# Gathering the tokens of a mixture-of-experts group in two halves of four experts, the second half behind gate and up of the first expert

## The reference

```python
def hierarchical_moe(x, w_group, b_group, w_router, b_router, w_gate, w_up, w_down):
    ...                                        # one group of 4, two experts of its 8, their weights
    combine = (group_onehot[:, :, None] * exp_w[:, None, :]).astype(x.dtype)
    y = jnp.zeros_like(xt)
    for g in range(N_GROUPS):
        h = jax.nn.silu(jnp.einsum('td,edf->tef', xt, w_gate[g])) * jnp.einsum('td,edf->tef', xt, w_up[g])
        y = y + jnp.einsum('tef,efd->td', h * combine[:, g, :, None], w_down[g])
    return y.reshape(B, S, D)
```

## Time and profile before

| | us |
|---|---|
| median of 3 runs | 1186.68 (1186.46 to 1187.39) |
| the profiled execution, its own time | 1187.27 |
| its span, first to last instruction | 1185.4 |
| PE busy | 877.0 (74%) |
| ACT busy | 239.7 (20%) |
| DVE busy | 208.7 (18%) |
| POOL busy | 18.9 (2%) |

### The profile page before, as it was taken

One profiled execution on the slowest core, in us unless ns is written; L12 is line 12 of the kernel. 1 busy time (PEld: TensorE's weight loads), 2 busy tenths in 40 slices (PEclk: granted clock), 3 DMA queues, 4 the chain that ended last, 5 costly groups with the idle time before them and its releaser, 6 DMA issues.

```text
span 1185.4 us, 18548 instructions
## 1 busy us (share of the span) xinstructions
PE 877.0 (74%) x7870; PEld 498.0 (42%) x7870; DVE 208.7 (18%) x516; ACT 239.7 (20%) x555; POOL 18.9 (2%) x38
## 2 busy tenths in 40 slices
PE   8999998668566856685677999866765676567655
PEld 4788564235223522352235556423422342234222
DVE  1022231120012001200112432212010201020112
ACT  2165432112001200120011324101200120012001
POOL 0000000000000000000001100000000000000000
PEclk9999999888889888988888999988988998899789
DMA  9922169999999999999999405999999999999994
GB/s 390 419 107 80 63 235 409 427 428 425 427 427 426 427 426 428 427 426 427 428 425 412 171 20 216 417 425 428 426 428 426 428 425 429 426 427 425 428 426 177
DMA packets 31054, 433.80 MB, mean 366 GB/s; under 512 B 3440, under 2 KB 3568, under 8 KB 4592
## 3 DMA queue, kind: packets, MB, share of 16 engines
q1 hardware_dynamic: 30816, 431.85, 86.8%
q10 hardware_dynamic: 144, 0.52, 0.1%
HBM read 431.31 MB, written 1.05 MB: 365 GB/s over the span
## 4 chain that ended last, share of the span: by engine, by line
DMA 46%; PE 44%; issue 4%; ACT 3%; DVE 2%; DVEq 0%; ACTq 0%; SPq 0%; POOLq 0%; POOL 0%
DMA ring<-in_w_moe 45%; PE ps L1278 9%; PE ps L1266 7%; PE ps L1149 5%; PE ps L1134 4%; PE ps L1322 4%; PE ps L1254 3%; PE ps L1109 2%; PE ps L1346 2%; PE ps L1078 2%; PE ps L1409 1%; ACT xT L645 1%; PE ps L1312 1%; PE ps L1227 1%; PE ps L1372 1%
## 5 line engine op out<-in xcount | busy, mean ns | idle before, releaser
L1278 PE MATMUL ps<-ring,xT 128*32 128x256 f32 x4096 | 283.9, 428 | 156.1 <-DMA ring<-in_w_moe 149.6
L1278 PEld LDWEIGHTS ps<-ring,xT 128*32 128x32 f32 x4096 | 135.8, 120 | 292.7 <-DMA ring<-in_w_moe 190.5
L1322 PE MATMUL ps<-ring,scr 128*32 128x256 f32 x2048 | 137.7, 414 | 39.0 <-DMA ring<-in_w_moe 26.7
L938 DVE TENSOR_TENSOR scr<-scr,ps 128x128 f32<-128x128 f32 x64 | 18.4, 288 | 536.6 <-ACT scr L653 536.6
L1322 PEld LDWEIGHTS ps<-ring,scr 128*32 128x32 f32 x2048 | 69.0, 118 | 92.2 <-ACT scr L655 32.9
L1266 PE MATMUL ps<-scr,xn 128*128 128x256 f32 x256 | 77.7, 468 | 38.7 <-issue 38.1
L653 ACT ACTIVATE scr<-ps 128x128 f32<-128x128 f32 x64 | 17.8, 278 | 382.2 <-PE ps L1278 382.2
L945 DVE COPY scr<-ps 32x256 f32<-32x256 f32 x128 | 53.3, 416 | 215.6 <-PE ps L1322 214.7
L659 ACT ACTIVATE scr<-ps 32x256 f32<-32x256 f32 x128 | 48.2, 377 | 178.0 <-PE ps L1322 177.3
L1266 PEld LDWEIGHTS ps<-scr,xn 128*128 128x128 f32 x256 | 58.6, 239 | 60.2 <-issue 47.4
L1254 PE MATMUL ps<-scr 128*128 128x512 f32 x128 | 62.0, 616 | 8.2 <-ACT scr L659 8.2
(11 more groups left out here) (142 smaller groups left out, 535.2 us busy)
## 6 DMA issues: line engine op xcount, KB each, us to landing
ring<-in_w_moe SPq DMA_DIRECT2D x192, 2048.0 KB, 32.8
ring<-in_w_a SPq DMA_DIRECT2D x7, 2048.0 KB, 28.0
ring<-in_w_b SPq DMA_DIRECT2D x4, 2048.0 KB, 40.0
ring<-in_w_a SPq DMA_DIRECT2D x2, 1024.0 KB, 9.0
h<-in_x SPq DMA_DIRECT2D x2, 512.0 KB, 4.7
ring<-in_w_b SPq DMA_DIRECT2D x1, 1024.0 KB, 41.1
out<-xn SPq DMA_DIRECT2D x4, 256.0 KB, 2.8
par<-in_small SPq DMA_DIRECT2D x1, 768.0 KB, 15.7
```

The lines of the kernel that those rows point to most:

```text
L1278: last = MM(ps[CAP * j:CAP * (j + 1), e % 2, 0:2 * P].rearrange("p (u f) -> p u f", u=2), xg[:, kk, CAP * e:CAP * (e + 1)], w[:, :, k, P * ...
L1322: last = MM(ps[CAP * c:CAP * (c + 1), 2 + b, 0:256], hT[:, b, CAP * j:CAP * (j + 1)], w[:, j, 256 * c:256 * (c + 1)], start=j == 0, stop=j ...
```

## The change

PE gathers four experts at a time: a block of the gather is now 128 columns wide, and there are 2 x 8 blocks in a group. The order on PE becomes: blocks 0 to 3 of experts 0 to 3, `gate_up(0, 0)`, blocks 4 to 7 of experts 0 to 3, `gate_up(0, 1)`, all eight blocks of experts 4 to 7, the transposes of `selw`, then expert 0's transpose and down and the other experts as before. ACT makes 16 copies of 128 columns in place of 8 of 256, still ahead of the copy to `selT` and of the first Silu. DVE builds `selg` in four instructions of 128 x 128 in place of two of 128 x 256, and signals after each pair.

```diff
@@ ACT, group
-                    for k in range(KD):
-                        act.wait_ge(xg_psum, it * KD + (k + 1))
-                        nc.scalar.activation(xg[:, k, :], ps[:, 6 + k % 2, 0:NE * CAP], ACT.Copy,
+                    for i in range(2 * KD):
+                        q, k = i // KD, i % KD
+                        act.wait_ge(xg_psum, it * (2 * KD) + (i + 1))
+                        nc.scalar.activation(xg[:, k, P * q:P * (q + 1)], ps[:, 6 + i % 2, 0:P], ACT.Copy,
                                              scale=gain[:, gi, k:k + 1]).then_inc(xg_done, 1)
                     act.wait_ge(selt_psum, it + 1)
@@ DVE, group
-                    slots = bc(iota.unsqueeze(1), 1, NE)
-                    for t in range(T):
-
-                        last = V.tensor_tensor(selg[:, t, :].rearrange("p (e s) -> p e s", e=NE),
-                                               slots, bc(rank[:, t, cols].unsqueeze(2), 2, CAP),
-                                               ALU.is_equal)
-                    last.then_inc(selg_done, 1)
-                    dve.wait_ge(selg_done, it + 1)
+                    slots = bc(iota.unsqueeze(1), 1, QUAD)
+                    for q in range(2):
+                        quad = bass.ds(g * NE + QUAD * q, QUAD)
+                        for t in range(T):
+                            last = V.tensor_tensor(
+                                selg[:, t, P * q:P * (q + 1)].rearrange("p (e s) -> p e s", e=QUAD),
+                                slots, bc(rank[:, t, quad].unsqueeze(2), 2, CAP), ALU.is_equal)
+                        last.then_inc(selg_done, 1)
+                    dve.wait_ge(selg_done, it * 2 + 2)
@@ PE, group
-                    pe.wait_ge(selg_done, it + 1)
                     pe.wait_ge(xn_done, T * (layer + 2))
-                    def gather(ks):
+                    def gather(q, ks):
+                        pe.wait_ge(selg_done, it * 2 + (q + 1))
                         for k in ks:
-                            if k >= 2:
-                                pe.wait_ge(xg_done, it * KD + (k - 1))
+                            i = KD * q + k
+                            if i >= 2:
+                                pe.wait_ge(xg_done, it * (2 * KD) + (i - 1))
                             for t in range(T):
-                                last = MM(ps[:, 6 + k % 2, 0:NE * CAP], xn[:, t, P * k:P * (k + 1)],
-                                          selg[:, t, :], start=t == 0, stop=t == T - 1)
+                                last = MM(ps[:, 6 + i % 2, 0:P], xn[:, t, P * k:P * (k + 1)],
+                                          selg[:, t, P * q:P * (q + 1)], start=t == 0, stop=t == T - 1)
                             last.then_inc(xg_psum, 1)
@@ PE, group, the order
-                    gather(range(KD // 2))
-                    pe.wait_ge(xg_done, it * KD + KD // 2)
+                    gather(0, range(KD // 2))
+                    pe.wait_ge(xg_done, it * (2 * KD) + KD // 2)
                     gate_up(0, 0)
-                    gather(range(KD // 2, KD))
+                    gather(0, range(KD // 2, KD))
+                    pe.wait_ge(xg_done, it * (2 * KD) + KD)
+                    gate_up(0, 1)
+                    gather(1, range(KD))
                     pe.wait_ge(selw_done, it + 1)
                     ...
-                    pe.wait_ge(xg_done, it * KD + KD)
                     for e in range(NE):
                         b = e % 2
+                        if e == QUAD:
+                            pe.wait_ge(xg_done, it * (2 * KD) + 2 * KD)
                         if e:
                             keep_warm(e, 0)
                             gate_up(e, 0)
                             keep_warm(e, 1)
-                        gate_up(e, 1)
+                            gate_up(e, 1)
```

## The result

| | kernel before | changed kernel |
|---|---|---|
| median | 1183.71 us (14 runs, 1179.51 to 1187.39) | 1189.68 us (14 runs, 1185.18 to 1193.42) |
| profiled execution, its own time | 1187.27 | 1188.93 |
| its span | 1185.4 | 1187.0 |

The ratio is 1.0052, 95% interval 1.0037 to 1.0068: the change costs 6.2 us (4.4 to 8.0). The forecast was 6.4. The two profiled executions differ by only 1.7 us; single executions of one kernel scatter over some 8 us, so the time of one is no measure here. What the profiles are good for is the distances within a stage, which repeat to a tenth of a us.

The account below looks back on a forecast made before the run. The weight stream, by its restart in each layer's first group, was taken to bound the kernel. Later load 3 (2.1) plus clock (1.1) gave 3.2 us a layer, 6.4 for two; on median 1186.7 that is 1193.1, range 1188.0 to 1196.5.

Parts of the forecast that it names:

- What bounds the kernel: MoE layers: weight stream at 427 GB/s bounds; each us on its virtual start is a us on the layer's end.
- The gather's own time and its pace: First group's gather: narrow blocks take 1.19 us a pair (bounds 0.89 and 1.37); PE's own time stays.
- rival (d): Narrow gather on PE: weight loads don't overlap, 0.25 us a record, + 9 us a layer, 1207; chance 0.02.
- What is moved: Expert 0, first group: Silu and table load lose their cover, load 3 issued at 187.8; +2.1 us a layer.
- Rival (c): First group: Silu or table load runs ahead of the last copies; each layer gains 3.0 us, 1180.7; chance 0.06.
- The table's price: ACT before expert 0's Silu: table load takes 1.28 us, the switch at most 0.2 beyond it.
- Rival (e): ACT, first Silu: table switch takes twice 1.28 us, load 3 1.3 later in either layer, 1195.7; chance 0.04.
- The clock: PE's gap before expert 0's down: clock falls, 1.1 us on down in each layer; bounds 0 and 1.4.
- Rival (a): Expert 0's down: the stall without the clock's fall, 2 x 2.1 us, 1190.9; chance 0.26.
- The model of the load: Stream restart: virtual start is the largest, over n, of issue n + 1.8 - 4.91 (n - 1).
- the spare time: Third load, layer 0: could be issued at 185.6 without moving the stream's start; 1.6 us to spare.
- The later groups: Groups after the first: five us later costs nothing, 19 are left; no hole in the stream.

Follow-up runs that it names:

- the kernel with 16 idle matmuls: Kernel before, plus 16 idle matmuls on PE ahead of expert 0's down in every group; ratio 1.0107, 12.7 us longer.
- the kernel with Silu early: Changed kernel with expert 0's Silu and its table load ahead of the second half's copies on ACT; ratio 0.9986 to the kernel before.
- (6): Kernel before, plus 6 idle matmuls on PE ahead of expert 0's down; ratio 0.9991, and 0.9994 when run again.
- the kernel with expert 0 first: Changed kernel with the gather of experts 4 to 7 and its copies moved behind expert 0's down; ratio 0.9961 to the kernel before.
- the split: Moved gather of experts 4 to 7 halved: four blocks behind expert 0's down, four behind expert 1's; ratio 0.9961 to the kernel before.

## Why the prediction was right, point by point

**What bounds the kernel.** Right in the main. The restart of the stream moved, and the sum of lags gives the time within the interval in nearly every kernel run. It also holds that a us of lag is a us on the layer's end: in layer 1, from the gather's start to the last down, the changed kernel takes 444.8 us where the kernel before takes 442.5, and its lag is 2.5 longer (the kernel with 16 idle matmuls is an exception, see the last section). "What follows the last slot is not touched" is not what the profiles show: the stretch between the layers in which PE issues nothing is 8.1 us instead of 6.2, in both profiles. Whether it reaches the time is not shown.

**The gather's own time and its pace.** Predicted 1.19 us for a pair of blocks; 1.16 to 1.17. Gate and up at + 2.82 and + 7.55; measured + 2.86 and + 7.51. Down at + 17.85; measured + 17.92 and + 17.86. The terms were taken from rows of the same shape in other stages, and they fit. Weights of 128 columns did load under running matmuls, 8 records in 1.09 us, or 0.14 with their wait for ACT: rival (d) would have needed 0.25.

**What is moved.** Right, and shown: the copy to `selT`, the table load and Silu, which lay under gate and up, came behind 16 copies and the transposes. Moving Silu alone takes the whole loss away. Rival (c) needed just this order and is the kernel with Silu early; it brought 1.7 us and not the 6 of (c), since load 3 then still decides (+ 15.4 + 2.0 + 1.8 - 9.8 = 9.4).

**The table's price.** The row of 1.28 us held. Silu began 0.02 after the load, and the switch cost what ACT_TABLE_LOAD's row says, now that nothing covers it. Rival (e) falls; the 2.66 us for a switch that the Trainium skill gives (ScalarE: Activation LUTs, What ACT_TABLE_LOAD costs) are not seen here either: from the end of selT's copy to Silu it was 1.31.

**The clock.** The kind was right, the size and place were not. I took 1.1 us in both layers; the fall cost 1.7 and 1.4 on down in layer 0 and nothing in layer 1, in both profiles. Rival (a) and the forecast each hold for one layer. The sum was hardly touched: 2.2 forecast, 1.4 to 1.7 found.

**The model of the load.** 1.8 us from issue to full rate was right where the queue had run dry: lags of 15.0 (16 idle matmuls), 10.7 (6) and 11.9 (changed kernel, layer 1) by the model, 14.7 to 14.9, 10.5 to 10.6 and 11.7 measured. The step that failed is the spare time, "the third load could be issued at 185.6 without moving S": a load issued 1.7 to 1.9 us ahead of the end of the one before still cost about 1 us. It did not matter for the forecast, as the changed kernel was past that edge, but in the lags it took nearly half of the gain from the kernel with expert 0 first (2.7 us against 5.0 with the split; in the time the two are equal).

**The later groups.** Right in the trace: in group 1 of the changed kernel down of expert 0 takes 3.46 us and starts at 292.5, and between 258 and 300 the rate is 426 GB/s:

```profile
258.00:300.00 42.00, 27.17 (x237) 16.76 (x237) 6.18 (x17) 11.03 (x26) 0.00 (x0) 0.80 1.01 426
```

**The number.** 1193.1 was 6.4 us above the median of the three runs that were shown; with 14 runs the median of the kernel before is 1183.7, and the changed kernel's 1189.7 lies 6.0 above it. That 6.4 came so close is in part luck: it was to be 3.2 us in either layer, and by the lags it was 3.7 in layer 0 and 2.2 in layer 1, since the clock cost more than its term in one and nothing in the other.

## What to carry to other kernels

Before moving work ahead of a wait, list what stands behind that work on every in-order engine: here 16 copies and a table load got between a finished product and the one instruction that turns it into a free buffer. Where a stream is the bound and stands still, find the buffers in the order in which they are freed, and put a time on each; a head start of the first two is worth nothing if the third comes late. And if a change that should shorten a stage lengthens it, move one instruction before giving it up: the same gather in halves, with expert 0 finished first, is 4.6 us faster than the kernel before.

## What the runs showed of the hardware that was not expected

- How far ahead the next transfer of 2 MB has to be issued: 1.9 us before the end of the running one was too late in layer 0 of the kernel with expert 0 first, where the rate dipped to 246 and 180 GB/s for a us each; 2.2 us before (load 2 of the changed kernel in layer 0, 175.8 against 178.0) it stayed at 377 to 442.
- The granted clock of PE fell to 1.2 GHz in or just behind a gap of 2.60 us in layer 0, and after the same gap it stayed at 2.4 in layer 1, in two executions of two. With five idle matmuls in the gap it stayed up in both layers of the one profile.
- The stretch in which PE issues nothing after a layer's loop of groups was 6.2 us in the profile of the kernel before, 8.1 in both of the changed kernel, 7.6 with expert 0 first, 11.8 with 16 idle matmuls and 6.0 to 6.6 in the other eight; it stands on the path between the layers. With 16 idle matmuls layer 1's last down came only 3.7 us later after its gather than before, where the lag says 5.6, so in that row of the table the longer stretch and this offset one another. None of these kernels was made to vary it, and it was not looked into.
